# Modulation rows of the second part: issued from ScalarE's DMA queue instead of SyncE's

## The chip, the cores and the metric

One Trainium2 chip, one of its cores. The metric is the device time of one execution in microseconds (us); lower is better. TensorE is called PE, VectorE DVE, ScalarE ACT, GpSimd POOL and SyncE SP, as the profile does.

## What is computed

One decoder layer over 256 tokens of width 2048: an mLSTM mixer and a gated MLP with a short convolution. Both take their input normalised and then modulated by a vector c. What matters here is the start of it:

```
sh1, sc1, g1, sh2, sc2, g2 = split(silu(c) @ w_mod + b_mod, 6)      # w_mod is 2048 x 12288
hm   = rms_norm(x) * (1.0 + sc1) + sh1                              # 256 x 2048
proj = hm @ w_in                                                    # q, k, v, o and the gates
...
```

So the first large product can't begin before columns of sc1 and sh1 are known, and each column of them takes all 2048 rows of w_mod.

## The kernel before

The product `hm @ w_in` goes over 16 blocks of 128 input columns (k), and over 12 strips of 512 output columns. It is cut in two passes. Pass 0 uses the first 6 blocks of k alone, in 12 strips of 3 steps, so 36 steps (`V_PASS1`); pass 1 adds the other 10 blocks. The reason for the cut is the modulation: the first part of it is the first 768 columns of sc1 and sh1 (16 loads into `m0`, L376, added by DVE in L1015 and by PE in L1442), and pass 0 needs only these. The second part is the other 1280 columns of sc1 and sh1: 2 x 16 loads of 128 x 1280 values (640 KB each) into six buffers `m1[0]` to `m1[5]`, L389. DVE adds them up while pass 0 runs (`add_m1`, L1024), and PE then sums over the partitions (`column_sums`, L1410).

A step of PE takes one weight half (512 KB of w_in, L402, into one of 8 places of `raw`): 12 matmuls, L1387 to L1389, on the two parts of the weight in float32r. For half v, ACT rounds it (`split_hi(v)`, `w_hi`, L613) and DVE takes the rest (`split_lo(v)`, `w_lo`, L985). The orders are written out by hand:

- ACT, at step p: waits for the end of PE's step p-1, then `split_hi(p + 3)`; at every third step it also takes a strip out of PSUM (`store_strip`, L691).
- DVE, at step p: `split_lo(p + 3)`, then `add_m1(p - 1)` for p from 1 to 32. An addition waits for its row to land and for the addition before it.
- PE, at step p: the 12 matmuls of half p; after step 24 and step 33 the first half of `column_sums` for sc1 and sh1, after steps 25 and 34 the second. The one after step 33 waits for all 32 additions.
- SP: the 16 loads into `m0`, halves 0 to 5, then in turn one row into `m1` and one half (row i before half 6 + i), then halves 38 to 40; before half 41 it waits for all 32 additions and loads the first row of the third modulation (L365).

SP waits for the free place before each load: a half for `split_lo` eight halves back, a row of `m1` from the sixth on for the addition of row i - 6:

```
elif i < 6:
    wait_m0((14, 14, 15)[i - 3])
else:
    sp.wait_ge(m1_used, i - 5)
```

Of the kernel before, what the change touches and what calls it, by code (L numbers as in the profile page):

```python
# [5 lines left out]
def hybrid_mlstm_convffn_adaln_kernel(nc, x_d, c_d, w_mod, b_mod, w_in, gate_bias, h_norm, w_out,  # L6
# [7 lines left out]
    P = 128  # L14
    SEQ, D = x_d.shape[1], x_d.shape[2]
    TB = SEQ // P
    KT = D // P
# [43 lines left out]
    MOD_ORDER = [C_SC1, C_SH1, C_G1, C_SC2, C_SH2, C_G2]  # L61
    M0_COLS, M1_COLS = K_FIRST * P, (KT - K_FIRST) * P
# [29 lines left out]
    with ExitStack() as ctx:  # L92
        def sem(name):
            return ctx.enter_context(nc.semaphore(name))
# [4 lines left out]
        def place(name, shape, offset, dt=f32):  # L99
            return nc.alloc_sbuf_tensor_at(name, shape, dt, offset=BASE + offset)  # L100
# [6 lines left out]
        m1 = [place(f"m1_{s}", [P, M1_COLS], (104 if s < 3 else 32) * KB + 4 * M1_COLS * (s % 3))  # L107
              for s in range(6)]
# [93 lines left out]
        m0_used, m0_summed = sem("m0_used"), sem("m0_summed")  # L202
        m1_in = [sem(f"m1_in{s}") for s in range(6)]
        m1_used = sem("m1_used")
# [20 lines left out]
        xn_made = sem("xn_made")  # L225
# [41 lines left out]
        def m0_adds(i):  # L267

            return (1,) if i % 2 == 0 else (0, 1)

        def m0_added(i):

            return sum(len(m0_adds(j)) for j in range(i + 1)), sum(2 - len(m0_adds(j)) for j in range(i + 1))
# [15 lines left out]
        def raw_half(v):  # L289

            s = (v - V_SIX) % 6 if V_SIX <= v < V_OUT else v % 8
            return raw[:, s // 2, (s % 2) * HALF:(s % 2 + 1) * HALF]

        def strip_of(vh):

            n = int(vh >= V_PASS1)
            m, kp = divmod(vh - n * V_PASS1, PAIRS[n])
            return n, n * STRIPS + m, n * PAIRS[0] + kp
# [22 lines left out]
        def wait_from_1(engine, semaphore, count):  # L321
            if count > 0:
                engine.wait_ge(semaphore, count)
# [14 lines left out]
        def _(sp):  # L338
# [28 lines left out]
            def wait_m0(i):  # L367
                added, summed = m0_added(i)
                sp.wait_ge(m0_used, added)
                sp.wait_ge(m0_summed, summed)  # L370

            def load_m0(i):
                n, rows = i // 8, 2 * (i % 8) * P
                if i >= 8:
                    wait_m0(i - 8)
                sp.dma_start(m0[:, i % 8, :].rearrange("p (j n) -> p j n", j=2),  # L376
                             w_mod[rows:rows + 2 * P, MOD_ORDER[n]:MOD_ORDER[n] + M0_COLS]
                             .rearrange("(j p) n -> p j n", p=P)).then_inc(m0_in[i % 8], 16)

            def load_m1(i):  # L380
                n, rows = i // KT, (i % KT) * P
                if i < 3:
                    sp.wait_ge(xn_made, TB)
                elif i < 6:
                    wait_m0((14, 14, 15)[i - 3])
                else:
                    sp.wait_ge(m1_used, i - 5)
                col = MOD_ORDER[n] + M0_COLS
                sp.dma_start(m1[i % 6][:], w_mod[rows:rows + P, col:col + M1_COLS])\  # L389
                  .then_inc(m1_in[i % 6], 16)  # L390

            def load_half(vh):
                n, m, kp = strip_of(vh)
                kind, j = PASS[n][m - n * STRIPS]
                col = STRIP_COL[kind] + QUARTER * j
                if vh < 8:
                    wait_m0((8, 9, 9, 10, 11, 11, 12, 13)[vh])
                elif vh < V_SIX + 6:
                    sp.wait_ge(raw_done, RAW0 + vh - 8 + 1)
                else:  # L400
                    sp.wait_ge(raw_done, RAW0 + vh - 6 + 1)
                sp.dma_start(raw_half(vh)  # L402
                             .rearrange("p (k n) -> p k n", k=2),
                             w_in[2 * kp * P:2 * (kp + 1) * P, col:col + QUARTER]
                             .rearrange("(k p) n -> p k n", p=P)).then_inc(half_in[vh % 8], 16)
# [15 lines left out]
                sp.dma_start(x[:, t, :], x_d[0, t * P:(t + 1) * P, :]).then_inc(x_in[t], 16)  # L421
            for i in range(16):
                load_m0(i)
            for vh in range(6):
                load_half(vh)
            for i in range(2 * KT):
                load_m1(i)
                load_half(6 + i)
            for vh in range(6 + 2 * KT, V_OUT):
                load_due_mods(vh)  # L430
                load_half(vh)
# [171 lines left out]
        def _(act):  # L603
            def split_hi(v, plus=0):

                if v >= 2 * N_UNITS:
                    return
                if v < V_OUT:
                    act.wait_ge(half_in[v % 8], 16 * (v // 8 + 1))
                elif v % 2 == 0:  # L610

                    act.wait_ge(raw_in[v // 2 % 4], 16 * ((v - V_OUT) // 8 + 1) + 2 * plus)
                nc.scalar.activation(w_hi[:, v % 4, :], raw_half(v), ACT.Copy).then_inc(w_hi_made, 1)  # L613

            def slot_hi(p):

                wait_from_1(act, half_done, p)
                split_hi(p + 3)
# [20 lines left out]
            def copy_xT0():  # L639
                for g in range(KT // 2):  # L640
                    act.wait_ge(xT_ready, g + 1)
                    nc.scalar.activation(xnT[:, 2 * g:2 * g + 2, :],
                                         ps[:, 4 + g % 4, :].rearrange("p (k t) -> p k t", k=2),
                                         ACT.Copy).then_inc(xT_copied, 1)

            def modulate_hi(n, first, last):

                for k in range(first, last):
                    nc.scalar.activation(hm_hi[:, k, :], xnT[:, k, :], ACT.Identity,
                                         bias=shift_p[:, k:k + 1], scale=scale_p[:, k:k + 1])\  # L650
                             .then_inc(hm_hi_made, 1)
# [14 lines left out]
            for n in range(2):  # L666
                col = MOD_ORDER[n]
# [11 lines left out]
            nc.scalar.activation(cvT[:], ps[:, 2, 0:4 * 2 * FT], ACT.Copy).then_inc(params_made, 1)  # L679
            copy_xT0()  # L680

            def scale_shift(n, count, src, out, plus_one):
                act.wait_ge(colsum_done, count)
                if plus_one:
                    nc.scalar.activation(out, src, ACT.Copy, bias=1.0).then_inc(sc_made, 1)
                else:
                    nc.scalar.activation(out, src, ACT.Copy).then_inc(sc_made, 1)

            def store_strip(m):
                for b in range(2):  # L690
                    nc.scalar.activation(strip_sums(0, m)[b], bank_heads(0, m, b), ACT.Copy)\  # L691
                             .then_inc(evac0, 1)

            def seed_strip(m):

                if m == STRIPS:
                    act.wait_ge(evac0, 2 * (STRIPS - 1))
                elif m == STRIPS + 1:
                    act.wait_ge(evac0, 2 * STRIPS)
                else:  # L700
                    act.wait_ge(evac1, 2 * (m - 1 - STRIPS))
                for b in range(2):
                    nc.scalar.activation(bank_heads(1, m, b), strip_sums(1, m)[b], ACT.Copy)\
                             .then_inc(seeded, 1)
# [48 lines left out]
                             .then_inc(kqT_copied, 1)  # L753

            split_hi(0)
            split_hi(1)
            scale_shift(0, 1, ps[:, SUM_BANK[0], 0:K_FIRST], scale_p[:, 0:K_FIRST], True)
            scale_shift(1, 2, ps[:, SUM_BANK[1], 0:K_FIRST], shift_p[:, 0:K_FIRST], False)
            act.wait_ge(sc_made, 2)
            act.wait_ge(xT_copied, K_FIRST // 2)  # L760
            for g in range(K_FIRST // 2):
                modulate_hi(0, 2 * g, 2 * g + 2)
                if g == 1:
                    split_hi(2)
            act.wait_ge(xT_copied, KT // 2)

            for p in range(V_PASS1):
                slot_hi(p)
                if p and p % PAIRS[0] == 0:
                    store_strip(p // PAIRS[0] - 1)  # L770
                    if p // PAIRS[0] == STRIPS - 1:
                        seed_strip(STRIPS)
                if p == V_PASS1 - 2:
                    scale_shift(0, 4, ps[:, SUM_BANK[0], K_FIRST:KT], scale_p[:, K_FIRST:KT], True)
                    scale_shift(1, 6, ps[:, SUM_BANK[1], K_FIRST:KT], shift_p[:, K_FIRST:KT], False)
                    act.wait_ge(sc_made, 4)
                if p >= V_PASS1 - 2:
                    k = K_FIRST + 2 * (p - (V_PASS1 - 2))
                    modulate_hi(0, k, k + 2)
# [145 lines left out]
            for n, tiles in enumerate(CHUNKS):  # L925
                with act.Fori(0, tiles // 2) as i:
                    for r in range(4):
# [3 lines left out]
                        col = 2 * i + (FT if r % 2 else 0) + pair  # L931
# [745 lines left out]
```

## Time and profile before

| what | value |
|---|---|
| median of 3 runs | 1192.72 us (1190.49 to 1193.34) |
| the profiled execution | 1189.14 us, its span 1187.4 us |
| PE busy | 1162.6 us (98% of the span) |
| DVE busy | 918.0 us (77%) |
| ACT busy | 632.0 us (53%) |
| DMA | 314.54 MB, mean 265 GB/s |
| mean granted clock of PE | 0.985 |

A share of busy time is a mean over stages with different limits. The change touches the stage from about 40 to 150 us of the span, so most rows below are of that stretch. Times in rows are us from the span's start unless marked ns. A row of the timeline gives start, length, engine, line, operation and shapes, how often, and in brackets how long the engine stood idle before it and what ended that. The q behind an engine's name is its sequencer, which issues DMAs.

### The profile page before, as it was taken

What the parts mean: (1) busy time and instruction counts of PE and PEld (TensorE: products, weight loads), DVE (VectorE), ACT (ScalarE), POOL (GpSimd) and SP (SyncE); (2) the same over time, 40 slices, a digit from 0 to 9 for tenths busy, and PEclk for the clock granted to TensorE, in tenths of its full rate; (3) what the DMA queues carried; (4) which work ended last, traced back from release to release, by engine and by line L of the source; (5) the groups of instructions that cost most, each with busy time, mean ns of one, the idle gap of its engine ahead of it and who ended that gap; (6) DMA issues with size and microseconds to landing.
All of it is one profiled execution on the core that took longest, in us unless ns stands there. A gap on an engine that the chain in (4) does not pass through costs nothing.

```text
span 1187.4 us, 17148 instructions
## 1 busy us (share of the span) xinstructions
PE 1162.6 (98%) x5890; PEld 995.6 (84%) x5890; DVE 918.0 (77%) x988; ACT 632.0 (53%) x919; POOL 160.5 (14%) x167
## 2 busy tenths in 40 slices
PE   5899999999999999999999999999999999999998
PEld 5788888888888888888888888888888888888887
DVE  5899877989988988988886446888885456777654
ACT  4355565666654556655554445555554455555442
POOL 0000030111122320212211000221220000121100
PEclk9599999999999998999999999999999999999999
DMA  9999989999999993988876578789775566766552
GB/s 362 398 402 401 396 288 328 363 404 400 345 357 363 406 290 107 257 240 229 252 225 207 182 228 232 212 243 249 214 232 192 195 194 182 196 189 179 207 174 77
DMA packets 260440, 314.54 MB, mean 265 GB/s; under 512 B 6208, under 2 KB 186888, under 8 KB 251688
## 3 DMA queue, kind: packets, MB, share of 16 engines
q1 hardware_dynamic: 259360, 312.51, 79.0%
q0 software_dynamic: 592, 1.22, 0.4%
q8 instruction: 28, 0.46, 0.2%
q10 hardware_dynamic: 442, 0.21, 0.1%
q14 instruction: 18, 0.15, 0.0%
HBM read 311.80 MB, written 2.11 MB: 264 GB/s over the span
## 4 chain that ended last, share of the span: by engine, by line
PE 95%; DMA 2%; DVE 1%; SPq 1%; POOL 0%; issue 0%; ACT 0%; DVEq 0%
PE ps L1300 27%; PE ps L1306 14%; PE ps L1340 9%; PE ps L1341 9%; PE ps L1342 9%; PE ps L1387 8%; PE ps L1389 7%; PE ps L1388 7%; DMA m<-in_l_w_mod_dram 2%; PE ps L1410 1%; SPq L376 1%; DVE acc L1015 0%; POOL small L548 0%; PE ps L1512 0%; PE ps L1466 0%; PE ps L1358 0%
## 5 line engine op out<-in xcount | busy, mean ns | idle before, releaser
L985 DVE TENSOR_TENSOR w_lo<-raw,w_hi 128x1024 fp32r<-128x1024 f32 x392 | 482.1, 1232 | 172.2 <-ACT w_hi L613 169.4
L613 ACT ACTIVATE w_hi<-raw 128x1024 fp32r<-128x1024 f32 x392 | 414.5, 1058 | 354.8 <-PE ps L1342 165.3
L1300 PE MATMUL ps<-hm,w_hi 128*128 128x512 f32 x1408 | 340.1, 392 | 1.7 <-DVE hm L1221 1.7
L1300 PEld LDWEIGHTS ps<-hm,w_hi 128*128 128x128 f32 x1408 | 258.3, 189 | 51.0 <-issue 1.9
L1306 PEld LDWEIGHTS ps<-hm,w_lo 128*128 128x128 f32 x1408 | 183.0, 191 | 8.4
L1306 PE MATMUL ps<-hm,w_lo 128*128 128x256 f32 x1408 | 185.3, 283 | 0.0
L1387 PE MATMUL ps<-w_hi,hm 128*128 128x512 f32 x384 | 153.3, 399 | 3.2 <-DVE hm L1035 2.7
L1389 PE MATMUL ps<-w_hi,hm 128*128 128x512 f32 x384 | 150.4, 392 | 0.0
L1388 PE MATMUL ps<-w_lo,hm 128*128 128x512 f32 x384 | 150.3, 391 | 0.0
L1342 PE MATMUL ps<-w_hi,act_lo 128*128 128x512 f32 x344 | 133.8, 389 | 0.0
L1341 PE MATMUL ps<-w_lo,act_hi 128*128 128x512 f32 x344 | 133.8, 389 | 0.0
L1340 PE MATMUL ps<-w_hi,act_hi 128*128 128x512 f32 x344 | 133.8, 389 | 0.0
L593 POOL TENSOR_TENSOR act_full<-conv_gate,conv_val 128x256 f32<-128x256 f32 x44 | 32.5, 738 | 555.4 <-DVE conv_val L1265 555.4
L940 ACT ACTIVATE up_sum<-ps 128x256 f32<-128x256 f32 x88 | 33.5, 380 | 105.5 <-PE ps L1300 104.2
L1387 PEld LDWEIGHTS ps<-w_hi,hm 128*128 128x128 f32 x384 | 72.7, 189 | 18.5 <-DVE hm L1035 2.8
L1389 PEld LDWEIGHTS ps<-w_hi,hm 128*128 128x128 f32 x384 | 72.5, 189 | 15.5
L1388 PEld LDWEIGHTS ps<-w_lo,hm 128*128 128x128 f32 x384 | 72.6, 189 | 14.7
L997 DVE SCALAR_TENSOR_TENSOR acc<-mod_raw,cT,acc 128x2048 f32<-128x2048 f32 x32 | 76.1, 2377 | 6.8 <-issue 4.4
L1342 PEld LDWEIGHTS ps<-w_hi,act_lo 128*128 128x128 f32 x344 | 64.6, 188 | 13.5
L1340 PEld LDWEIGHTS ps<-w_hi,act_hi 128*128 128x128 f32 x344 | 64.6, 188 | 13.5
L1341 PEld LDWEIGHTS ps<-w_lo,act_hi 128*128 128x128 f32 x344 | 64.6, 188 | 13.3
L597 POOL TENSOR_TENSOR act_lo<-act_full,act_hi 128x256 f32 x44 | 65.0, 1478 | 23.7 <-DVE act_hi L1272 23.7
(176 smaller groups left out, 1092.0 us busy)
## 6 DMA issues: line engine op xcount, KB each, us to landing
raw<-in_l_w_up_dram SPq DMA_DIRECT2D x88, 1024.0 KB, 5.8
raw<-in_l_w_in_dram SPq DMA_DIRECT2D x96, 512.0 KB, 11.9
mod_raw<-in_l_w_mod_dram SPq DMA_DIRECT2D x48, 1024.0 KB, 7.7
raw<-in_l_w_down_dram SPq DMA_DIRECT2D x44, 1024.0 KB, 5.0
m<-in_l_w_mod_dram SPq DMA_DIRECT2D x32, 640.0 KB, 13.8
raw<-in_l_w_out_dram SPq DMA_DIRECT2D x16, 1024.0 KB, 8.9
m<-in_l_w_mod_dram SPq DMA_DIRECT2D x16, 768.0 KB, 13.2
mod_third<-in_l_w_mod_dram SPq DMA_DIRECT2D x8, 1024.0 KB, 8.3
```

Of the source, the lines that this page charges most:

```text
L597: nc.gpsimd.tensor_tensor(act_lo[:, part], act_full[:, k, :], act_hi[:, part].bitcast(f32), ALU.subtract)\
L613: nc.scalar.activation(w_hi[:, v % 4, :], raw_half(v), ACT.Copy).then_inc(w_hi_made, 1)
L985: nc.vector.tensor_tensor(w_lo[:, v % 4, :], raw_half(v), w_hi[:, v % 4, :].bitcast(f32), ALU.subtract)\
L997: nc.vector.scalar_tensor_tensor(out=part, in0=src, scalar=cT[:, ds(tile, 1)], in1=part, op0=ALU.mult, op1=ALU.add).then_inc(mod_done, 1)
L1300: return mm(ps[:, 4 + w % 4, :], w_hi[:, v % 4, j * P:(j + 1) * P], both, start=(k == 0), stop=stop, skip_group_check=True)
L1306: return mm(ps[:, 4 + w % 4, 0:SEQ], w_lo[:, v % 4, j * P:(j + 1) * P], hm_hi[:, k, :], start=False, stop=stop, skip_group_check=True)
L1340: mm(out, s_hi, hi, start=first, stop=False, skip_group_check=True)
L1341: mm(out, s_hi, lo, start=False, stop=False, skip_group_check=True)
L1342: last = mm(out, s_lo, hi, start=False, stop=final, skip_group_check=True)
L1387: mm(out, s_hi, hi, start=(k == 0), stop=False, skip_group_check=True)
L1388: mm(out, s_hi, lo, start=False, stop=False, skip_group_check=True)
L1389: last = mm(out, s_lo, hi, start=False, stop=(k == final), skip_group_check=True)
```

## The change

SP no longer loads `m1`. It issues halves 6 to 37 with nothing between them. ACT issues the 32 rows on its own queue: rows 0 and 1 right behind `split_hi(0)` and `split_hi(1)`, rows 2 to 5 together ahead of step 0, and row p + 3 at step p behind `slot_hi(p)` for p from 3 to 28. The places, sizes and waits of each row are as before, with ACT waiting where SP did.

```
-            for vh in range(6):
+            for vh in range(6 + 2 * KT):
                 load_half(vh)
-            for i in range(2 * KT):
-                load_m1(i)
-                load_half(6 + i)
...
+            def load_m1(i):
+                n, rows = i // KT, (i % KT) * P
+                if i < 3:
+                    act.wait_ge(xn_made, TB)
+                elif i < 6:
+                    added, summed = m0_added((14, 14, 15)[i - 3])
+                    act.wait_ge(m0_used, added)
+                    act.wait_ge(m0_summed, summed)
+                else:
+                    act.wait_ge(m1_used, i - 5)
+                col = MOD_ORDER[n] + M0_COLS
+                act.dma_start(m1[i % 6][:], w_mod[rows:rows + P, col:col + M1_COLS])\
+                   .then_inc(m1_in[i % 6], 16)
...
             split_hi(0)
+            load_m1(0)
             split_hi(1)
+            load_m1(1)
...
             act.wait_ge(xT_copied, KT // 2)
+            for i in range(2, 6):
+                load_m1(i)
 
             for p in range(V_PASS1):
                 slot_hi(p)
+                if 3 <= p < 2 * KT - 3:
+                    load_m1(p + 3)
```

## Rows read from the trace of the kernel before

**Rows 1.** The page's busy time: us, share of the span, instructions.

```profile
PE 1162.6 (98%) x5890; PEld 995.6 (84%) x5890; DVE 918.0 (77%) x988; ACT 632.0 (53%) x919; POOL 160.5 (14%) x167
```

**Rows 2.** Waits of PE, whole span: us in total, times, longest.

```profile
...
PE ps L1387 <- DVE hm L1035: 2.7, 1, 2.7
...
PE ps L1387 <- issue: 0.5, 1, 0.5
```

**Rows 3.** The chain that ended last, 42 to 60 us: start, us, what.

```profile
27.87 14.26 DMA m<-in_l_w_mod_dram
...
44.28 2.73 PE ps L1410 x12
...
49.69 0.80 PE ps L1387
```

**Rows 4.** Busy time by engine in a window; last PEclk, DMA share, GB/s.

```profile
60.00:100.00 40.00, 40.00 (x178) 33.11 (x177) 39.51 (x30) 20.79 (x25) 0.00 (x0) 1.00 1.04 401
```

**Rows 5.** DMA issues, 60 to 140 us: count, KB each, median us to landing.

```profile
DMA packets 11315, 32.11 MB, mean 401 GB/s; under 512 B 885, under 2 KB 901, under 8 KB 11310
...
m<-in_l_w_mod_dram SPq DMA_DIRECT2D x25, 640.0 KB, 13.9
raw<-in_l_w_in_dram SPq DMA_DIRECT2D x28, 512.0 KB, 13.3
acc<-in_l_b_mod_dram POOLq DMA_DIRECT2D x1, 8.0 KB, 5.1
```

**Rows 6.** Lengths of DMA issues: chain before 42 us, then timelines of SP and ACT.

```profile
5.08 3.70 SPq L376
...
99.46 2.08 SPq L389 DMA_DIRECT2D m<-in_l_w_mod_dram  x1
...
3.95 1.53 ACTq L669 DMA_DIRECT2D acc<-in_l_b_mod_dram  x2
```

**Rows 7.** Row 23 of m1, half 28 and half 40: issue, then us to landing.

```profile
L389 SPq DMA_DIRECT2D m<-in_l_w_mod_dram x1: 467/467/467, 105.0 to 105.0; - x1
...
DMA to landing us min/median/max: 14.5/14.5/14.5
...
L402 SPq DMA_DIRECT2D raw<-in_l_w_in_dram x1: 651/651/651, 104.3 to 104.3; - x1
...
DMA to landing us min/median/max: 13.6/13.6/13.6
...
L402 SPq DMA_DIRECT2D raw<-in_l_w_in_dram x1: 1984/1984/1984, 135.4 to 135.4; - x1
...
DMA to landing us min/median/max: 12.8/12.8/12.8
```

**Rows 8.** Timeline of ACT: halves 0, 28 and 31 split, one strip stored.

```profile
43.51 1.06 ACT L613 ACTIVATE w_hi<-raw 128x1024 fp32r<-128x1024 f32 x1 [18.34 <-DMA raw<-in_l_w_in_dram]
...
118.17 1.06 ACT L691 ACTIVATE o_acc<-ps 128x512 f32<-128x512 f32 x2
119.93 1.06 ACT L613 ACTIVATE w_hi<-raw 128x1024 fp32r<-128x1024 f32 x1 [0.69 <-PE ps L1389]
...
130.37 1.06 ACT L613 ACTIVATE w_hi<-raw 128x1024 fp32r<-128x1024 f32 x1 [0.69 <-PE ps L1389]
```

**Rows 9.** Timeline of DVE: half 28, row 24, halves 31 and 35, row 31.

```profile
121.02 1.22 DVE L985 TENSOR_TENSOR w_lo<-raw,w_hi 128x1024 fp32r<-128x1024 f32 x1
122.45 1.55 DVE L1024 SCALAR_TENSOR_TENSOR acc<-m,cT,acc 128x1280 f32<-128x1280 f32 x1 [0.21 <-DMA m<-in_l_w_mod_dram]
...
131.46 1.22 DVE L985 TENSOR_TENSOR w_lo<-raw,w_hi 128x1024 fp32r<-128x1024 f32 x1
...
142.34 1.22 DVE L985 TENSOR_TENSOR w_lo<-raw,w_hi 128x1024 fp32r<-128x1024 f32 x1
143.49 1.54 DVE L1024 SCALAR_TENSOR_TENSOR acc<-m,cT,acc 128x1280 f32<-128x1280 f32 x1
```

**Rows 10.** Timeline of PE: the column sums that wait for all additions.

```profile
146.49 1.17 PE L1410 MATMUL ps<-ones,acc 128*128 128x1 f32 x10
```

More of the change, by code:

```diff
@@ L378, in load_m0 @@
                              .rearrange("(j p) n -> p j n", p=P)).then_inc(m0_in[i % 8], 16)
[L380 to L390, printed above, removed]
             def load_half(vh):
```

## The prediction

> **What bounds the kernel now.** I read the page first, then PE's waits, then the chain of waits for the start, then windows and timelines of the stretch that the change touches.
>
> The page shows PE busy for 98% of the span [rows 1]. Where an engine is that full, a change elsewhere can gain only what PE idles. The list of PE's waits shows how little that is from 50 us on: 0.5 us by issue in this stretch, and the wait of 2.7 us before the first step [rows 2]. The chain of the start shows what sets that first step: the last load into m0 takes until 27.87 + 14.26 = 42.1 us, the first columns are summed over partitions at 44.28, and the first matmul of pass 0 runs at 49.69 [rows 3]. Up to there DMA is the bound, by bytes.
>
> From then on three things run almost level, and this is what the reader is to see. PE is busy for 40.00 of 40 us, DVE for 39.51 of 40, and the DMA engines for all of it, at 401 GB/s [rows 4]. A step takes 2.72 us: four steps of DVE are 142.34 - 131.46 = 10.88 us [rows 9]. In each step one half and one row are wanted, 512 and 640 KB [rows 5]; at 401 GB/s that is 1.31 + 1.63 = 2.94 us. So DMA falls back by 0.22 us a step and lives on the lead that it had. The lead is nearly used up where the column sums give some back: row 23 was issued at 105.0 and landed 14.5 us later at 119.5, just as its addition was due, and row 24 made DVE wait for 0.21 us [rows 7, 9]. Half 28 landed at 104.3 + 13.6 = 117.9 us and ACT took it at 119.93, so its margin is 2.0 us [rows 7, 8]. PE saw none of this.
>
> **The change part by part.** *The bytes stay.* 32 rows and the same halves pass through the same DMA engines, which have no idle time in this stretch [rows 4]. Only the order changes, and who waits.
>
> *Taken from SP:* 32 issues, each with up to 2.08 us [rows 6]. SP computes nothing and its queue is held up by transfers, not by issuing, so this is worth 0 us. Halves may now be asked for earlier, up to the eight places.
>
> *Before PE begins:* row 0 is issued behind the split of half 0, at 43.51 [rows 8]; the last load into m0 has landed by then (42.1), so the chain of the start isn't touched. Row 1 is issued between the split of half 1 and the first scale. An issue on ACT's queue took 1.53 / 2 = 0.77 us [rows 6]; ACT is still in the split of 1.06 us, and the second column sums end at 44.28 + 2.73 = 47.0, so this is hidden: 0 us. If it were not hidden, it would cost 0.77 us once.
>
> *Rows 2 to 5 in one go*, at about 50.5 us: 4 x 0.77 = 3.1 us before ACT gets to step 0. That puts the split of half 3 at some 53.6 us at the latest. Half 3 is wanted by PE three steps after 49.69 (the first of them at half clock, so its 0.80 us row stands for longer matmuls): not before 49.69 + 3 x 2.72 = 57.9 us. The split and the rest of it take 1.06 + 1.22 us [rows 8, 9], so it is ready at 55.9 and 2 us are left. 0 us.
>
> *Rows 6 to 31, one a step:* ACT has 2.72 us a step, uses 1.06 for the split and, every third step, 1.06 for a strip [rows 8], and an issue adds 0.77: 2.89 us in one step of three, 1.83 in the others, 2.18 on average. Issues are the sequencer's and can overlap the engine's work. 0 us. The wait for a free place stands now on ACT, with the strip's store and the next split queued behind it. Row p + 3 at step p wants the addition of row p - 3; DVE did it one step earlier. So it holds only if DVE is over 1.6 us late (a step of 2.72 less the rest of its addition), which the next part prices.
>
> *The order of the bytes* is the real question. Before, row v - 6 stood ahead of half v. Now rows have a queue of their own. The rows of before show that another queue doesn't stand behind SP's: an 8 KB load from POOL landed in 5.1 us where SP's own needed 13.3 to 13.9 [rows 5]. So rows will land sooner, and halves pay for it. How the engines share the two queues no row shows; three cases bound it.
>
> - *One and one* (a row, a half, a row, ...): from row 2 on, row v - 3 comes with half v, three rows earlier than before. That is 3 x 1.63 = 4.9 us later for half v. Half 28 had 2.0 us of margin and comes 2.9 us late. DVE starts it at 121.02 + 2.9 = 123.9, goes on without idling at 2.72 a step, gets to half 35 after 7 steps at 142.9, and ends the last addition 1.15 + 1.54 us later, at 145.6. PE's column sums come at 146.49 [rows 9, 10]. PE itself needs half 28 when ACT splits half 31, at 130.37 [rows 8]; it is ready at 125.1. No stall: 0 us, with 0.9 us to spare.
> - *Rows first:* every row that is asked for lands before the halves behind it. At most rows v - 5 to v - 1 are then ahead, 5 x 1.63 = 8.2 us. Half 28 comes 6.2 us late, is split off by 128.4 (PE wants it at 130.37), and the same sum puts the last addition at 121.02 + 6.2 + 19.0 + 2.7 = 148.9 us. PE stalls 2.4 us before the column sums.
> - *Even by bytes:* a row then takes 640 KB at 200 GB/s = 3.27 us, more than a step, so rows fall back by 0.55 us a step and DVE waits for rows. The end of that is known: SP stops after half 40 until all additions are made, and all of these bytes had landed by 135.4 + 12.8 = 148.2 us [rows 7]. With 1.54 us of addition that is 149.8, a stall of 3.3 us.
>
> A stall here is not given back, since PE waits for nearly nothing afterwards [rows 2].
>
> I take one and one, because a row and a half differ little in size and each goes as one request to all engines. The Trainium skill, page "DMA: Bandwidth & Descriptors", section "Queues, rings and completion order", says that each DMA engine goes round its queues a packet at a time, with some 9 to 17 descriptors in a packet. By that rule a row and a half would pass roughly in turn, so it gives the same 0 us; no row of before shows two large queues side by side. The same page, section "Issuing engines are not separate DMA queues", says that transfers started from several engines interleave on the same 16 and only issue time is saved. It speaks against a gain in bandwidth by the change; the trace agrees as far as the 401 GB/s with no idle time go [rows 4].
>
> **The sum:** 0 for the issues, 0 for the order, between 0 and +3.3 us at its ends, and at most -0.5 us if PE's one idle spot at the second pass's start went away. Against the profiled execution that is 1189.14 + 0. That execution is 3.6 us under the median of the runs shown, 1192.72; against the median I forecast 1192.7, say 1193.
>
> **Rivals.**
>
> *1. The queues share unevenly and DVE is late at the column sums.* For it: DVE has 39.51 of 40 us filled [rows 4] and can't catch up. Against: the column sums after steps 24 and 25 give it some 2 us back. Time: +2.4 to +3.3 us, 1195 to 1196. Still within what can be told from no change.
>
> *2. ACT's queue blocks as SP's did (slower).* The issue itself can take long: 3.70 us at 5.08 and 2.08 us at 99.46 on SP [rows 6], when five to seven large loads were under way. If ACT's issue waited likewise, ACT would need 2.08 + 1.06 + 0.35 = 3.49 us a step, 0.77 over PE's 2.72; over the 26 rows of steps 3 to 28 that is 20 us, of which the lead of three steps hides some 6 and the column sums 2, so +12 us: 1205. The point from which it decides is an issue of 2.72 - 1.41 = 1.31 us. The burst alone, 4 x 3.70 = 14.8 us, would put half 3 at 67.6 against 57.9: up to +9.7. Against: only rows are in ACT's queue, at most six of 640 KB, and two 8 KB issues went out in 0.77 us each while SP's was filling [rows 6].
>
> *3. It gains.* For it: halves are asked for sooner, DVE loses its 0.21 us wait, and fewer loads queue in one place. Against: PE has 0.5 us to give in this stretch [rows 2]. To gain 0.3% something later must move, for which I see no step; 1189 at best.
>
> **How the numbers follow.** A measurement of this kernel tells a difference of about 0.3%, 3.6 us, from none. The forecast has 0.70 (1193; by itself 1190.5 to 1194.5, the spread of the runs), rival 1 has 0.15, rival 2 has 0.09, rival 3 has 0.06. Rival 1 ends within 0.3%, but a fifth of it may pass the bound with a share still less even. So faster 0.06, same 0.82, slower 0.12. The range takes in rival 1's +3.3 on the median and the lowest run: 1189.5 to 1197.0. It leaves out rival 2.
>
> **What the profile would show.** Right: rows land on ACT's queue in well under 13.9 us; halves come later than now and ACT waits for some of them; DVE shows waits in the rows of half 16 on; the column sums still begin near 146.5; issues on ACT of under 1 us; 401 GB/s as now; PE without a wait between 50 and 150 us. Wrong: PE idle before L1410 near 146 us (rival 1); ACT's issues of over 1.3 us and PE waiting for w_lo (rival 2); a first step off 49.7 us, or a gap that shows up past 150 us, where I looked least. The step that would make it wrong is the share between the queues.

## The result, and the profile after

The changed kernel took 1193.21 us (median of 20 runs, 1190.51 to 1196.9), the kernel before 1191.60 us (20 runs, 1190.02 to 1193.34). The ratio is 1.0018, with a 95% interval of 1.0012 to 1.0025: slower by some 2 us, inside the 0.3% that I called no change, but not nothing. The profiled execution of after took 1190.51 us with a span of 1188.8 us, which is the fastest of its 20 runs. So its profile shows the mildest form of what happens; a second profile of the same kernel, below, shows the usual one.

The page of after, busy time and DMA queues. q1 is SP's queue, q10 is ACT's; the last number is the share of 16 engines over the span:

```profile
PE 1163.8 (98%) x5890; PEld 996.6 (84%) x5890; DVE 917.0 (77%) x988; ACT 631.6 (53%) x919; POOL 159.0 (13%) x167
...
q1 hardware_dynamic: 254752, 291.53, 74.5%
q10 hardware_dynamic: 5050, 21.18, 4.5%
```

The DMA issues of after from 60 to 140 us, beside [rows 5]:

```profile
DMA packets 11452, 32.05 MB, mean 401 GB/s; under 512 B 893, under 2 KB 909, under 8 KB 11448
...
m<-in_l_w_mod_dram ACTq DMA_DIRECT2D x26, 640.0 KB, 6.8
raw<-in_l_w_in_dram SPq DMA_DIRECT2D x28, 512.0 KB, 19.5
```

The same 32 MB pass at the same 401 GB/s. A row of the modulation now lands in 6.8 us and not 13.9, a half in 19.5 us and not 13.3. Who pays, the reader sees in the waits of ACT from 54 to 147 us (us in total, times, longest), first before, then after:

```profile
ACT w_hi L613 <- PE ps L1389: 48.1, 33, 2.8
```

```profile
ACT w_hi L598 <- DMA raw<-in_l_w_in_dram: 28.1, 19, 3.4
ACT w_hi L598 <- PE ps L1394: 17.2, 12, 3.0
ACT w_hi L598 <- DVE acc L1029: 3.5, 1, 3.5
```

The last line looks like ACT held up by a full place in `m1`, but it is one more late half. It is the wait before half 27, and ACT had issued its row behind half 26 at once, at 117.00. Half 27 was issued at 100.3 and landed 21.1 us later, at 121.4, and ACT took it at 121.52. An addition of DVE ended at 121.48 by chance.

Half 28 in after (its issue and us to landing), then its split on ACT and on DVE, then the last addition and PE's column sums, to be read against [rows 7 to 10]:

```profile
L390 SPq DMA_DIRECT2D raw<-in_l_w_in_dram x1: 368/368/368, 103.1 to 103.1; - x1
...
DMA to landing us min/median/max: 21.0/21.0/21.0
```

```profile
124.21 1.06 ACT L598 ACTIVATE w_hi<-raw 128x1024 fp32r<-128x1024 f32 x1 [0.66 <-DMA raw<-in_l_w_in_dram]
```

```profile
125.30 1.23 DVE L990 TENSOR_TENSOR w_lo<-raw,w_hi 128x1024 fp32r<-128x1024 f32 x1
...
146.03 1.55 DVE L1029 SCALAR_TENSOR_TENSOR acc<-m,cT,acc 128x1280 f32<-128x1280 f32 x1
```

```profile
147.63 1.28 PE L1415 MATMUL ps<-ones,acc 128*128 128x1 f32 x10 [0.36 <-DVE acc L1029]
```

It landed at 103.1 + 21.0 = 124.1 us, 6.2 us later than before. ACT took it 4.3 us later (124.21 against 119.93), DVE too (125.30 against 121.02). DVE got some of that back, and ended the last addition at 147.58, where before it was 143.49 + 1.54 = 145.03: 2.55 us later. PE waited for it by 0.36 us.

### The profile page after: what moved, and what is told of

It reads as the page before. It is cut to its first block, busy times and chain, and to the rows that moved or that the text cites. A ratio compares the mean times of both kernels' runs of the same rounds, so it can differ in the third digit from the quotient of the medians.

```text
span 1188.8 us, 17148 instructions
## 1 busy us (share of the span) xinstructions
PE 1163.8 (98%) x5890; PEld 996.6 (84%) x5890; DVE 917.0 (77%) x988; ACT 631.6 (53%) x919; POOL 159.0 (13%) x167
## 4 chain that ended last, share of the span: by engine, by line
PE 88%; DMA 8%; DVE 2%; issue 1%; SPq 1%; ACT 1%; POOL 0%; DVEq 0%; ACTq 0%
PE ps L1305 27%; PE ps L1311 14%; PE ps L1345 9%; PE ps L1347 9%; PE ps L1346 9%; PE ps L1392 5%; DMA raw<-in_l_w_in_dram 5%; PE ps L1394 5%; PE ps L1393 5%; DMA m<-in_l_w_mod_dram 2%; PE ps L1415 1%; SPq L376 1%; DVE acc L1029 1%; ACT w_hi L598 0%; DVE acc L1020 0%
## 5 line engine op out<-in xcount | busy, mean ns | idle before, releaser
L1393 PEld LDWEIGHTS ps<-w_lo,hm 128*128 128x128 f32 x384 | 72.8, 190 | 14.8
```

Source lines behind the costliest of these rows:

```text
L1393: mm(out, s_hi, lo, start=False, stop=False, skip_group_check=True)
```

## The experiments

Every edit but those of act_small and late2 is made to the changed kernel. Ratios are to the kernel before, which ran on the same chip beside each group of four. Waits are those of PE before the column sums after step 33, in the one profiled execution of each kernel; the medians are over 4 to 12 executions.

| kernel | median, us | ratio (95%) | wait of PE, us |
|---|---|---|---|
| before_again | 1190.33 | 1.0004 (0.9994 to 1.0013) | 0 |
| after_again | 1193.5 | 1.0025 (1.0016 to 1.0035) | 1.6 |
| ahead1 | 1191.59 | 1.0005 (0.9996 to 1.0013) | 0 |
| ahead2 | 1192.33 | 1.0014 (1.0005 to 1.0022) | 0 |
| act_small | 1191.42 | 1.0005 (0.9996 to 1.0014) | 0 |
| burst_only | 1190.05 | 0.9991 (0.9983 to 1.0000) | 0 |
| steady_only | 1193.37 | 1.0023 (1.0014 to 1.0031) | 0.5 |
| dve_light | 1191.06 | 1.0004 (0.9996 to 1.0013) | 0 |
| late2 | 1193.38 | 1.0027 (1.0015 to 1.0039) | 1.4 |
| pieces2 | 1193.85 | 1.0028 (1.0018 to 1.0039) | 1.4 |
| gap2 | 1190.8 | 1.0008 (0.9998 to 1.0017) | 0 |
| gap4 | 1205.11 | 1.0122 (1.0108 to 1.0137) | 4.4 |

### after_again and before_again: the two kernels once more

No edit.

> The changed kernel once more, as a yardstick for this group. Theory (rows are served first, halves come late, DVE is late at the column sums after step 33): ratio to before 1.001 to 1.0025, half 28 lands 5 to 7 us later than before, the last row's addition ends 2 to 4 us later than before and PE waits for it by 0.3 to 3 us. Rival (the profiled execution's 1.4 us longer span is spread over the whole run and has nothing to do with the rows): no wait of PE before the column sums, or one that doesn't match the difference of the times.

> The kernel before against itself: a yardstick for how far a measurement tells from no change, and a second profile of it. All theories: ratio 0.999 to 1.001, PE without a wait before the column sums after step 33. Open: whether its attention stage (244 to 354 us) is the quick one of the first profile (107.5 us for the same matmuls) or the one of 109.8 us that the one-ahead kernel's profile has.

The wait of PE in after_again, the last addition and the column sums:

```profile
PE ps L1415 <- DVE acc L1029: 1.6, 1, 1.6
```

```profile
146.46 1.55 DVE L1029 SCALAR_TENSOR_TENSOR acc<-m,cT,acc 128x1280 f32<-128x1280 f32 x1
```

```profile
148.06 1.68 PE L1415 MATMUL ps<-ones,acc 128*128 128x1 f32 x10 [1.62 <-DVE acc L1029]
```

Then after_again in windows of 4 us; the third number from the end is the granted clock, 1.00 being 2.4 GHz and 0.50 being 1.2:

```profile
144.00:148.00 4.00, 2.44 (x11) 1.69 (x9) 4.00 (x4) 3.96 (x7) 0.00 (x0) 1.00 0.66 246
148.00:152.00 4.00, 3.94 (x16) 3.45 (x17) 2.28 (x3) 0.00 (x0) 0.00 (x0) 0.60 0.73 244
152.00:156.00 4.00, 4.00 (x16) 3.32 (x14) 0.00 (x0) 0.00 (x0) 0.00 (x0) 0.55 0.92 317
156.00:160.00 4.00, 3.47 (x17) 2.68 (x17) 2.58 (x5) 3.54 (x7) 3.24 (x4) 1.00 1.01 397
```

This is what I had nowhere in my sum. PE stands for 1.6 us, and then its clock is granted at 1.2 GHz for most of the 8 us from 148 on. The first matmul of the second pass tells the price. It is the one after the short idle spot; first before_again, then after, then after_again:

```profile
154.82 0.47 PE L1387 MATMUL ps<-w_hi,hm 128*128 128x512 f32 x1 [0.52 <-issue]
```

```profile
156.17 0.47 PE L1392 MATMUL ps<-w_hi,hm 128*128 128x512 f32 x1 [0.52 <-issue]
```

```profile
159.76 0.47 PE L1392 MATMUL ps<-w_hi,hm 128*128 128x512 f32 x1 [0.53 <-issue]
```

From the start of the column sums to this matmul it is 8.4 us in before_again and in before (there 154.88 - 146.49 [rows 10]), 156.17 - 147.63 = 8.5 in after, and 159.76 - 148.06 = 11.7 in after_again. So the wait of 1.6 us is followed by 3.3 us lost at half clock, where the wait of 0.36 us was followed by none. The second pass begins 4.9 us later than in before_again; by the end of the span 1191.8 - 1188.9 = 2.9 us are left. Some 2 us come back from 440 us on: between 440 and 460 us the granted clock was 1.00 in after_again and 0.74 in before_again; why, I didn't test.

The span of one profile can't price the change by itself, since the rest of it varies by as much. From the first matmul of the second pass to the end it is 1031.8 to 1035.5 us in all profiles but gap4's (the two of before: 1032.5 and 1034.1). The question left open in the expectation is part of it. From that matmul to the column sums that begin between 442 and 448 us it is 287.6 to 287.9 us in before, before_again, after, after_again, pieces2, gap2, dve_light and late2, and 289.9 to 290.5 in ahead1, ahead2, act_small, burst_only and steady_only. These five, and only they, show PE's weight loads waiting for DVE in the attention stage, here ahead1 from 244 to 354 us:

```profile
PEld ps L1517 <- DVE gated L1134: 2.6, 6, 0.5
```

No run shows what brings this longer form or how often each kernel takes it. burst_only has it in its profile, at 1191.83 us the slowest of its 11 executions, which speaks against its being in all of them. Compared are therefore the medians, and the times up to the second pass.

### ahead1 and ahead2: rows asked for later

The rows that stood ahead, one or two instead of three. ahead1 (ahead2 has 5, 2 and p + 2 in these places):

```
-            for i in range(2, 6):
+            for i in range(2, 4):
                 load_m1(i)
...
-                if 3 <= p < 2 * KT - 3:
-                    load_m1(p + 3)
+                if 3 <= p < 2 * KT - 1:
+                    load_m1(p + 1)
```

> Rows are issued one ahead (row p + 1 at step p) instead of three. Theory: two rows fewer stand before a half, 2 x 1.63 = 3.3 us; half 28 then lands some 3 us later than before, ACT gets it about 1 us late, the column sums give that back, PE has no wait before them, and the time is that of before (ratio 0.9995 to 1.0008), if the rows still land within the 7.7 us that are left to them (they took 6.7). Rival (the cost lies in the issue on ACT or in having two queues at all): ratio as the changed kernel's, 1.0018.

> Rows issued two ahead (row p + 2 at step p). Theory: one row fewer before a half than three ahead, 1.6 us; DVE's last addition ends some 1 us after that of before, at 146 to 147, at the edge of PE's wait. Wait of 0 to 0.8 us, mostly too short for the clock to fall: ratio 1.000 to 1.0015, between one ahead (1.0005) and three ahead (1.0018 to 1.0025).

The last addition and the column sums of ahead1, then the last addition of ahead2:

```profile
143.56 1.54 DVE L1029 SCALAR_TENSOR_TENSOR acc<-m,cT,acc 128x1280 f32<-128x1280 f32 x1
```

```profile
146.56 1.17 PE L1415 MATMUL ps<-ones,acc 128*128 128x1 f32 x10
```

```profile
144.86 1.55 DVE L1029 SCALAR_TENSOR_TENSOR acc<-m,cT,acc 128x1280 f32<-128x1280 f32 x1
```

One ahead, the last addition is where it was before and the time is back, with the rows still on ACT's queue. Two ahead, it ends at 146.41, in the middle. Issue cost and the second queue as such are thereby out as causes. The last addition ends at 145.10, 146.41 and, three ahead, 147.58 to 148.01 us: 1.2 to 1.6 us for each row that is asked for earlier. For ahead2 the profile shows no wait, but its ratio is above 1. Its column sums came at 147.08 in this profile (its clock rose late at the start, as in after) against an addition that ended at 146.41; where PE comes at 146.4, as in before_again, nothing is left. That other executions of it wait is my reading, not shown; its profile also has the longer attention stage.

### act_small: the issues alone

The kernel before, with 32 extra loads of 8 bytes a partition from ACT at the places of the change (the calls, which stand where the change has them, aren't shown):

```
+            def load_m1(i):
+                if i >= 6:
+                    act.wait_ge(spare_in[i % 6], 16 * (i // 6))
+                act.dma_start(spare[:, 2 * (i % 6):2 * (i % 6) + 2], w_mod[(i % KT) * P:(i % KT + 1) * P, 0:2])\
+                   .then_inc(spare_in[i % 6], 16)
```

> The kernel before, rows loaded by SP as before, and 32 extra loads of 128 x 2 values (8 bytes a partition, into spare columns that nobody reads) issued by ACT at the places where the changed kernel issues its rows. Prices the issues and the second queue without moving the rows' bytes. Theory (issues cost nothing): ratio 0.9995 to 1.0007, PE without a wait before the column sums. Rival (issues on ACT, or their waits, hold up the splits): ratio 1.0015 or more, ACT's issues over 1 us.

An issue took 0.33 us, half of what I had allowed:

```profile
63.45 0.34 ACTq L687 DMA_DIRECT2D spare<-in_l_w_mod_dram  x1
```

The issues cost nothing that the ratio of 1.0005 (0.9996 to 1.0014) could show. The small packets weren't quite free: with 3744 of them between 60 and 140 us the stream ran at 392 GB/s and not 401, and DVE waited 4.1 us in all for rows. That too ended without a wait of PE.

### burst_only and steady_only: which part of the change

burst_only leaves rows 0 to 5 to ACT and gives rows 6 to 31 back to SP; steady_only does the opposite. The core of burst_only (its expectation stands second):

```
-            for vh in range(6 + 2 * KT):
+            for vh in range(12):
                 load_half(vh)
+            for i in range(6, 2 * KT):
+                ...
+                sp.wait_ge(m1_used, i - 5)
+                sp.dma_start(m1[i % 6][:], ...)
+                load_half(6 + i)
...
-                if 3 <= p < 2 * KT - 3:
-                    load_m1(p + 3)
```

> Rows 0 to 5 are left on SP's queue, in turn with halves 6 to 11; rows 6 to 31 are issued by ACT three ahead. Theory (what counts is how many rows are asked for ahead of a half while the stage lasts, not the burst at its start): halves are early at first and then come as late as in the changed kernel from about half 16 on; last addition after 146.5, ratio 1.001 to 1.003. Rival (the burst of the first six rows does the harm): ratio below 1.0008, no wait of PE before the column sums.

> The other part: rows 0 to 5 are issued by ACT as in the changed kernel, rows 6 to 31 by SP, each ahead of half 6 + i as before. Theory: halves 5 to 8 land a few us later than before, the rest as before since everything stands in one queue again; last addition near 145, no wait of PE, ratio 0.9995 to 1.001. Rival as in the run of the other part: ratio 1.0015 or more.

Last additions, burst_only first, and PE's column sums in steady_only:

```profile
143.21 1.54 DVE L1034 SCALAR_TENSOR_TENSOR acc<-m,cT,acc 128x1280 f32<-128x1280 f32 x1
```

```profile
146.75 1.55 DVE L1037 SCALAR_TENSOR_TENSOR acc<-m,cT,acc 128x1280 f32<-128x1280 f32 x1
```

```profile
148.35 1.28 PE L1423 MATMUL ps<-ones,acc 128*128 128x1 f32 x10 [0.50 <-DVE acc L1037]
```

The burst does no harm, and the steady stream has the whole effect in the medians. In the profile of steady_only PE came late to the column sums, waited only 0.5 us and kept its clock: its second pass begins at 156.84 us, 2.0 us later than in before_again, and its longer attention stage comes on top. burst_only is even 0.9991 of before, with an interval that ends at 1.0000; I wouldn't call it faster on that.

### dve_light: room for DVE to catch up

The changed kernel, additions of rows 8 to 31 over half of the columns:

```
+                cols = M1_COLS if i < 8 else M1_COLS // 2
-                part = acc[:, n, M0_COLS:D]
+                part = acc[:, n, M0_COLS:M0_COLS + cols]
-                nc.vector.scalar_tensor_tensor(out=part, in0=m1[i % 6][:],
+                nc.vector.scalar_tensor_tensor(out=part, in0=m1[i % 6][:, 0:cols],
```

> The changed kernel, but DVE adds only half of the columns of rows 8 to 31 (640 of 1280; the left-out columns' modulation isn't complete). Rows and halves land as in the changed kernel. Theory (late halves hurt only because DVE has no room to catch up before the column sums after step 33): DVE catches up 0.6 us in each step, the last addition ends before PE needs it, PE has no wait there and keeps the full clock; ratio 0.9993 to 1.0007, though ACT still waits for halves by DMA for over 20 us. Rival (late halves reach PE directly, through w_hi and w_lo): PE waits in L1392 to L1394 and the ratio stays at 1.002 or more.

Its waits of ACT from 54 to 147 us, and its last addition:

```profile
ACT w_hi L598 <- DMA raw<-in_l_w_in_dram: 36.7, 22, 3.5
```

```profile
145.16 0.88 DVE L1030 SCALAR_TENSOR_TENSOR acc<-m,cT,acc 128x640 f32<-128x640 f32 x1
```

ACT waits for halves even more than in after, and PE has no wait before the column sums. So late halves reach PE through DVE's queue of work alone. The kernel leaves out half of the columns of these rows, so its output is not that of the layer; only its timing counts.

### late2: the wait without the loads

The kernel before, two extra additions of DVE into free row places ahead of the last one:

```
+                if i == 2 * KT - 1:
+                    for j in (1, 2):
+                        nc.vector.scalar_tensor_tensor(out=m1[(i - j) % 6][:], in0=m1[i % 6][:],
+                                                       scalar=cT[:, 0:1], in1=m1[i % 6][:],
+                                                       op0=ALU.mult, op1=ALU.add)
```

> The kernel before (rows on SP's queue, no change of any load), with two extra additions of DVE into row places that are free by then, right ahead of the last one: 2 x 1.54 us. Its last addition then ends near 148.2 instead of 145.1, so PE waits some 1.6 us before the column sums after step 33, as in the changed kernel, without any change in the loads. Theory (PE's wait for the last addition, and the fall of PE's clock behind it, are the whole price): the granted clock falls to about half for some 6 us after the wait, the end of the stage moves by the wait plus some 3 us, 4 to 5.5 us in all, ratio 1.003 to 1.005. Rival (the clock's fall has another cause, in DMA or ACT): clock stays 1.0, ratio 1.001 to 1.0018.

PE's wait, the column sums, the clock behind them and the first matmul of the second pass:

```profile
PE ps L1415 <- DVE acc L1029: 1.4, 1, 1.4
```

```profile
149.13 1.27 PE L1415 MATMUL ps<-ones,acc 128*128 128x1 f32 x10 [1.36 <-DVE acc L1029]
```

```profile
148.00:152.00 4.00, 2.87 (x17) 2.56 (x18) 3.35 (x3) 1.31 (x3) 0.00 (x0) 0.94 0.46 131
152.00:156.00 4.00, 4.00 (x18) 3.42 (x17) 0.00 (x0) 0.10 (x1) 0.07 (x1) 0.63 0.93 313
```

```profile
159.23 0.47 PE L1392 MATMUL ps<-w_hi,hm 128*128 128x512 f32 x1 [0.52 <-issue]
```

No load is moved, and wait, half clock and time are like those of the change: 1.0027 (1.0015 to 1.0039) against 1.0018 to 1.0025. The fall cost less here, 159.23 - 149.13 - 8.4 = 1.7 us, and the second pass begins 4.4 us later than in before_again, within the 4 to 5.5 that I expected; the ratio came in a little under the 1.003 that I expected at least. A late last addition, and what PE's clock does after it, are enough for the price of the change, and no experiment shows another part of it.

### pieces2, gap2 and gap4: how the queues share

Rows in smaller packets. pieces2 asks for two adjacent pieces, gap2 and gap4 put 16 and 8 columns between two and four, so their places in `m1` are 1312 columns long and DVE reads them with the gaps (an addition still takes 1.55 us in gap2). The load in gap2:

```
-                act.dma_start(m1[i % 6][:], w_mod[rows:rows + P, col:col + M1_COLS])\
+                act.dma_start(m1[i % 6][:, :, 0:M1_COLS // 2],
+                              w_mod[rows:rows + P, col:col + M1_COLS]
+                              .rearrange("p (j n) -> p j n", j=2))\
...
```

> Each row is loaded in two pieces of 640 columns in one request, so that its packets are 2560 bytes beside the halves' 2048, instead of 5120. Theory (the queues take turns by packet, so a queue's share of the bytes goes by the size of its packets): while both queues are full, rows get 2560 / 4608 = 56% in place of 70%, a row takes 2.9 us in place of 2.3 between 50 and 62 us, halves land some 1 to 3 us earlier than in the changed kernel, and the wait before the column sums goes: ratio 0.9995 to 1.001. Rival (shares don't depend on packet size): row 0 to 5 land 2.3 us apart as before this edit, ratio 1.0018.

> The changed kernel with each row landing in two pieces of 640 columns that lie 16 columns apart, so that they can't be merged: packets of 2560 bytes beside the halves' 2048. (The earlier edit in two adjacent pieces left the packets as they were: 3745 on ACT's queue between 62 and 145 us.) Theory (turns by packet): some 7000 packets there; between 50 and 62 us rows get 56% of the bytes and not 66%, row 4 lands at 63 and not at 60.3. Later, when only some rows are asked for at a time, rows still land in under 9 us, and the halves come only 0.5 to 1 us sooner, so the wait of PE shrinks from 1.6 to about 1 us and the ratio lies between 1.0005 and 1.002. Rival (the share doesn't go by packet size): rows 0 to 5 land as in the changed kernel, ratio 1.002 to 1.003.

> The same with four pieces of 320 columns, 8 columns apart: packets of 1280 bytes. Theory (turns by packet): rows get 1280 / 3328 = 38% while both queues are full, some 4.3 us a row, less than the 2.72 us of a step allow; rows fall back, DVE waits for rows by DMA (over 3 us in all from about row 12 on), halves are early until SP has no free place, and the last row lands as late as the bytes allow, up to 148.2: PE waits 1 to 3.3 us before the column sums, ratio 1.001 to 1.005. Rival (share not by packet size): as the changed kernel, no wait of DVE for rows.

pieces2 said nothing on this. ACT's queue from 62 to 145 us (packets, MB, share of 16 engines), in pieces2 and then in gap2:

```profile
q10 hardware_dynamic: 3745, 17.04, 51.3%
```

```profile
q10 hardware_dynamic: 7384, 17.76, 56.1%
```

The 3745 packets of pieces2 are as many as in after, so it is the changed kernel a third time, with 1.4 us of wait. The queues between 50 and 62 us, while both are full (packets, MB, share of 16 engines), in after, gap2 and gap4:

```profile
q10 hardware_dynamic: 690, 3.13, 65.1%
q1 hardware_dynamic: 877, 1.68, 37.3%
```

```profile
q10 hardware_dynamic: 1094, 2.64, 57.8%
q1 hardware_dynamic: 1092, 2.10, 46.4%
```

```profile
q10 hardware_dynamic: 1737, 2.16, 51.3%
q1 hardware_dynamic: 1230, 2.36, 54.2%
```

Rows of 5120-byte packets got 3.13 / 4.81 = 65% of the bytes, of 2560 bytes 56%, of 1280 bytes 48%. One packet in turn would give 71, 56 and 38%. So the share follows the size of the packet, but not in strict turns at the ends. The last addition of gap2:

```profile
145.09 1.55 DVE L1031 SCALAR_TENSOR_TENSOR acc<-m,cT,acc 128x1280 f32<-128x1280 f32 x1
```

It ended at 146.6 us, 0.9 us earlier than in after, and the ratio is 1.0008 (0.9998 to 1.0017). From 62 to 145 us its rows landed in 12.6 us, not in the under 9 that I expected, and still none came late for DVE; ACT waited for halves by 8.5 us in all, against 28.1. I had expected some 1 us of wait and there was none, but in this profile PE reached the column sums only at 147.59. Where PE comes at 146.4, 0.2 us would be left.

gap4 turned into something else. In ACT's timeline the issue itself takes long, with ACT idle behind it:

```profile
49.29 5.10 ACTq L678 DMA_DIRECT2D m<-in_l_w_mod_dram  x1
...
54.49 4.04 ACTq L678 DMA_DIRECT2D m<-in_l_w_mod_dram  x1
58.57 2.01 ACT L598 ACTIVATE w_hi<-raw 128x1024 fp32r<-128x1024 f32 x2 [6.82 <-issue]
```

From 71 us on every issue took 1.5 to 4.2 us. From 62 to 145 us rows landed in 16.2 us and halves in 7.1; from 50 to 62 us the stream ran at 377 GB/s instead of 402. PE waited 4.4 us before the column sums and 3.5 us for strips that ACT stored late, and the kernel took 14.8 us more: 1.0122, where I had put it at 1.005 at most. Late rows and a blocked ACT come together in this run, and it doesn't tell their shares.

## Why the prediction was right, and where not

*What bounds the kernel*: right. PE's first matmul came at 49.74 us against 49.69, DMA ran at 401 GB/s, DVE had no room.

*The issues*: right at 0 us, and shown by act_small and ahead1; one took 0.33 to 0.40 us where I had 0.77. The burst of rows 2 to 5 went out at 47.4 to 49.2 us, not at 50.5, and cost nothing (burst_only).

*The order of the bytes*: this step failed. I took "one and one", three rows more ahead of half 28 and 2.9 us of lateness, with 0.9 us to spare. Measured were 6.2 us of later landing (3.8 rows) and 4.3 us of lateness after the margin of 2.0. The case that happened is the one that I called "rows first" and gave 0.15 as rival 1; it had 8.2 us, 6.2 of lateness and a last addition at 148.9, a little too much of each. The signs say the same: PE idle before the column sums, which I had named for rival 1, is what came, and they began at 147.6 and 148.1 us, not near 146.5. I chose by the size of the requests (640 and 512 KB), which in turns would give rows 56% of the bytes; measured were 65% while both queues were full. The rule that I cited, from the Trainium skill, page "DMA: Bandwidth & Descriptors", section "Queues, rings and completion order", led me the same way; the measurement decides against that reading. What counted was the size of the packets (5120 and 2048 bytes). [rows 5] had it: 11310 - 901 = 10409 packets of 2 to 8 KB for 25 rows and 28 halves are 128 packets a row and some 257 a half, if a row is one packet a partition.

*A stall is not given back*: half right. The wait of 0.4 to 1.6 us is what I priced as 2.4, but I left out what follows it, up to 3.3 us lost at half clock. Together they are 4.9 us at the start of the second pass in after_again, and some 2 us of that came back later through the clock. The net is 1.6 and 3.0 us in medians (3.4 in pieces2), 0 in my sum and 2.4 to 3.3 in rival 1. So the forecast of no change held by luck: the case that happened was small, and the mechanism that I forecast was not the one at work.

*Rival 2* (ACT's queue blocks) didn't occur in the changed kernel, where no issue took over 0.40 us, but gap4 shows that it is real, with issues of up to 5.10 us and +14.8 us. That this is near my +12 is in part chance, since gap4 also has late rows and a slower stream. It has 512 packets a row where the change has 128 and gap2 256; that the number of outstanding packets decides is my reading, not shown. *Rival 3* (a gain) found nothing: no kernel with the steady part on ACT has a median below that of before.

*Spread*: the runs of after scatter more (1190.5 to 1196.9) than those of before. In the three profiles of this kernel PE is ready for the column sums at 147.3 us (after), 146.4 (after_again) and 146.3 (pieces2); the granted clock from 50 to 56 us was 0.58, 0.73 and 0.76, so PE comes earlier where its clock rose earlier. The last addition ends at 147.6 to 148.0 in all three. An early PE waits longer, and in these profiles only the long waits, 1.6 and 1.4 us, were followed by half clock. late2 has PE ready as late as 147.8 us and lost its clock too, after a wait of 1.4 us. That this explains the whole scatter isn't shown; the two forms of the attention stage and the clock near 450 us add to it in every kernel.

## What to carry to other kernels

Here the DMA engines were full, and a second queue made no bandwidth (401 GB/s before and after); it only changed who was served first, and the queue with the larger packets got the larger share (65% for 5120 bytes against 2048). Before moving a load to a queue of its own, look for the work behind the other queue that has the least slack: here DVE, busy for 39.5 of 40 us, was 4.3 us late at half 28 and still 2.55 us late at the last addition. Ask for the moved rows as late as they can still land (one step ahead was enough here). And price a wait of PE with the clock that it may lose, not by its length alone.

## What the hardware showed that I had not expected

- The share of two full queues went with the packet size: 65, 56 and 48% of the bytes for packets of 5120, 2560 and 1280 bytes against 2048.
- Smaller packets cost bandwidth while the engines stayed busy: 401 GB/s as the kernel before loads, 392 with 3744 packets of 8 bytes between, 394 with rows in 2560-byte packets and 376 with rows in 1280-byte packets (from 62 to 145 us).
- After waits of PE of 1.4 us (late2) and 1.6 us (after_again) in the midst of full work its granted clock was 1.2 GHz for a part of the next 8 us (windows of 4 us: 0.94 and 0.63, 0.60 and 0.55), costing 1.7 and 3.3 us; after waits of 0.4 and 0.5 us (after, steady_only) it stayed at 2.4 GHz.
- A request for two adjacent pieces of each partition's row made as many packets as one for the whole row (3745 from 62 to 145 us); with a gap of 16 columns between the pieces in the destination there were 7384.
